# Hybrid attention and mixture-of-experts layer: the down weights' loads move to ScalarE's queue

## What is computed

```
gates  = softmax over the 4 largest router logits of each token, 0 elsewhere     (256 x 32)
for each expert e:                                    wgu 1024 x 2048, wd 1024 x 1024
    hgu  = xt @ wgu[e] + bgu[e]
    gate = min(hgu[:, :1024], 7);  up = clip(hgu[:, 1024:], -7, 7)
    y    = ((up + 1) * gate * sigmoid(1.702 * gate)) @ wd[e] + bd[e]
    acc += gates[:, e] * y
out = rmsnorm(h + acc)
```

## Time and profile before

| | |
|---|---|
| median of 3 runs | 1243.33 us (1241.56 to 1244.72) |
| the profiled execution | 1241.16 us, span 1239.3 us |
| TensorE matmuls busy | 1121.8 us (91% of the span) |
| VectorE, ScalarE, GpSimd busy | 205.8, 167.0, 18.6 us |
| bytes moved by DMA | 437.11 MB, mean 353 GB/s over the span |
| SyncE's queue | 434.19 MB; ScalarE's queue 1.57 MB |
| mean granted TensorE clock | 0.987 |

### The profile page before, as it was taken

How to read it: one execution, slowest core, us unless ns; L and a number is a source line. 1 busy time by engine, 2 the same in 40 slices (tenths; PEclk the granted TensorE clock), 3 DMA queues, 4 the chain that set the end, 5 groups by cost and what they waited for, 6 DMA issues and landing times.

```text
span 1239.3 us, 15513 instructions
## 1 busy us (share of the span) xinstructions
PE 1121.8 (91%) x6044; PEld 444.4 (36%) x6044; DVE 205.8 (17%) x420; ACT 167.0 (13%) x326; POOL 18.6 (1%) x68
## 2 busy tenths in 40 slices
PE   7999999958999999999999999999999998898885
PEld 6676444433333332323333233333333332322321
DVE  1301222141112111111111111111111111111111
ACT  2274222140000000000000000000000000000002
POOL 1010000000000000000000000000000000000000
PEclk9999999978999999999999999999999999999998
DMA  9922123338999999999999999999999999999994
GB/s 334 386 75 109 51 111 140 135 136 333 407 417 418 418 417 418 418 417 418 418 419 418 417 418 418 418 417 418 417 418 417 417 417 417 417 418 418 417 418 194
DMA packets 86628, 437.11 MB, mean 353 GB/s; under 512 B 7704, under 2 KB 7760, under 8 KB 53744
## 3 DMA queue, kind: packets, MB, share of 16 engines
q1 hardware_dynamic: 84880, 434.19, 86.3%
q10 hardware_dynamic: 1424, 1.57, 0.5%
q0 software_dynamic: 304, 1.06, 0.2%
HBM read 435.74 MB, written 1.06 MB: 352 GB/s over the span
## 4 chain that ended last, share of the span: by engine, by line
SPq 47%; PE 37%; DMA 9%; issue 4%; DVE 2%; ACT 1%; DVEq 0%
SPq L315 26%; SPq L310 20%; PE bank L1019 10%; DMA ring<-in_w_gate_up_dram 7%; PE bank L862 7%; PE bank L859 5%; PE bank L1049 3%; PE bank L945 2%; PE bank L956 2%; DMA ring<-in_w_down_dram 2%; PE bank L1002 2%; PE bank L993 1%; PE bank L917 1%; PE bank L839 1%; PE bank L1038 0%
## 5 line engine op out<-in xcount | busy, mean ns | idle before, releaser
L1019 PE MATMUL bank<-ring,gates 128*64 128x512 f32 x2048 | 476.9, 604 | 18.2 <-DMA ring<-in_w_gate_up_dram 15.3
L1049 PE MATMUL bank<-ring,gates 128*64 128x512 f32 x1024 | 244.2, 603 | 60.0 <-DMA ring<-in_w_down_dram 59.9
L1019 PEld LDWEIGHTS bank<-ring,gates 128*64 128x64 f32 x2048 | 135.1, 137 | 276.9 <-issue 191.3
L771 DVE TENSOR_SCALAR gates<-bank 128x512 f32<-128x512 f32 x32 | 22.1, 691 | 790.2 <-PE bank L1019 790.2
L1049 PEld LDWEIGHTS bank<-ring,gates 128*64 128x64 f32 x1024 | 64.0, 136 | 238.8 <-DMA ring<-in_w_down_dram 152.8
L862 PE MATMUL bank<-ring,colsT 128*128 128x512 f32 x192 | 85.0, 597 | 0.0
L1002 PE MATMUL bank<-gates,scatter_w 64*128 64x512 f32 x256 | 63.6, 615 | 0.8 <-ACT gates L570 0.7
L566 ACT ACTIVATE gates<-gates 128x512 f32<-128x512 f32 x32 | 20.2, 630 | 296.6 <-DVE gates L771 296.6
L859 PE MATMUL bank<-colsT,ring 128*128 128x256 f32 x256 | 58.8, 388 | 0.0
L993 PEld LDWEIGHTS bank<-onehot,qkT 128*128 128x128 bf16 x1536 | 47.7, 99 | 27.9 <-issue 25.2
L570 ACT ACTIVATE gates<-bank 128x512 f32<-128x512 f32 x32 | 19.1, 597 | 260.9 <-PE bank L1049 260.9
(11 more groups left out here) (167 smaller groups left out, 500.3 us busy)
## 6 DMA issues: line engine op xcount, KB each, us to landing
ring<-in_w_gate_up_dram SPq DMA_DIRECT2D x256, 1024.0 KB, 20.6
ring<-in_w_down_dram SPq DMA_DIRECT2D x128, 1024.0 KB, 24.6
ring<-in_w_in_dram SPq DMA_DIRECT2D x10, 2048.0 KB, 18.7
ring<-in_w_out_dram SPq DMA_DIRECT2D x1, 4096.0 KB, 14.1
ring<-in_w_proj_sb_dram SPq DMA_DIRECT2D x1, 2048.0 KB, 7.6
ring<-in_w_proj_moba_dram SPq DMA_DIRECT2D x1, 2048.0 KB, 13.4
resid<-in_x_dram SPq DMA_DIRECT2D x2, 512.0 KB, 3.7
bias<-u_scratch POOLq DMA_DIRECT2D x1, 1024.0 KB, 12.4
```

Source lines behind the costliest of these rows:

```text
L771: V.tensor_scalar(gate_t, bank[4][:, :], SWIGLU_LIMIT, None, ALU.min).then_inc(gate_rd, 1)
L1019: ins = mm(bank[4 + i][SLOTS * c:SLOTS * (c + 1), :], xeT[:, k, :], ring[:, k, i * D + c * CH:i * D + (c + 1) * CH], start=False, stop=k = ...
L1049: ins = mm(bank[6][SLOTS * c:SLOTS * (c + 1), :], rows, ring[:, KD + s, j * D + c * CH:j * D + (c + 1) * CH], start=k == 0, stop=k == KD - 1)
```

## The change

Down loads of experts 1 to 31 are issued by ScalarE, in its loop, behind `expert_rows` of the expert before. Four are issued one after the other, behind the copy of y, which itself waits for all four down slots. SyncE keeps expert 0's twelve loads and all gate-up loads. In a further pass, which doesn't happen with these data, SyncE would load expert 0's down weights as before. Two helpers with the slot and the source rows are shared by both engines.

```diff
+        dn = w_down[0].rearrange("e (k c p) n -> e k p c n", p=P, c=2)
+
+        def down_slot(s):
+            return ring[:, s, :].rearrange("p (c n) -> p c n", c=2)
+
+        def down_rows(e, s):
+            return (dn[e, s - KD] if isinstance(e, int)
+                    else dn[bass.ds(e, 1), s - KD].rearrange("o p c n -> p (o c) n"))
...
             def load_slot(e, s):
...
-                    dst = ring[:, s, :].rearrange("p (c n) -> p c n", c=2)
-                    src = (dn[e, s - KD] if isinstance(e, int)
-                           else dn[bass.ds(e, 1), s - KD].rearrange("o p c n -> p (o c) n"))
-                    sp.dma_start(dst, src).then_inc(slot_in[s], 16)
+                    sp.dma_start(down_slot(s), down_rows(e, s)).then_inc(slot_in[s], 16)
...
                 load_gate_up(1, done)
                 with sp.Fori(1, E - 1) as e:
                     load_gate_up(e + 1, done)
-                    load_down(e, done)
-                load_down(E - 1, done)
...
                     gate_sigmoid(e + done)
                     expert_rows(e + (done - 1))
+                    for s in range(KD, RING):
+                        act.dma_start(down_slot(s), down_rows(e, s)).then_inc(slot_in[s], 16)
                 hidden_columns(done + (E - 1))
```

More of the change, by code:

```diff
@@ L303, in _ @@
             gu = w_gate_up[0].rearrange("e (k p) n -> e k p n", p=P)
-            dn = w_down[0].rearrange("e (k c p) n -> e k p c n", p=P, c=2)
             def load_slot(e, s):
```

## The result

The changed kernel takes 1305.7 us (median of 4 runs, 1303.54 to 1308.78) against 1243.82: a ratio of 1.0499 (95% interval 1.0479 to 1.0520), 62 us slower. The profiled execution has a span of 1301.8 us, 62.5 more than before. Most of the loss lies where the prediction saw none, inside the periods.

What follows compares the result with a forecast made beforehand. The prediction took the saturated DMA engines (418 GB/s, 30.1 us an expert) as the bound. Its terms, 13.7 us at the end (1.4 of the first expert included) and 1 for the clock, summed to +14.7: 1258 us, range 1247 to 1285.

Steps and rivals of the forecast that it cites:

- ScalarE's issues: In each expert, ScalarE's four issues, some 2 us, vanish in its idle 6.5 us after copying y: cost 0.
- rival C: ScalarE's issues held up like SyncE's, 4.02 us each, delaying token weights: +97 us, 1355 us; chance 0.03.
- Later issue, no gap: Between 400 and 1214 us, later down issues cost 0, as four or five gate-up loads are still to come.
- step 3: Inside the periods, down loads get half the bandwidth beside gate-up loads and land in time: cost 0.
- rival A: Inside the periods, down loads get a third; 1 to 2.5 us lost in each of 27: 1285 to 1325 us; chance 0.12.
- twelve small gaps: TensorE's waits per expert, said to become one of 3 to 4 us before the last gate-up slot, without moving the period.
- The rate: DMA rate of the mixed stream stays at 418 GB/s, no change, with 1% either way (8 us of 814).
- Rival B: In the saturated stream, the rate rises, up to 434 GB/s: 30 us back over 27 periods, 1228 us; chance 0.10.
- First expert: At the first moved down loads, near 330 us, the DMA engines stand idle for 1.4 us: +1.4 us.
- Last expert: At the end, expert 31's down loads are asked for late, last landing 1235.7 instead of 1222.0: +13.7 us, first expert's term included.
- The 1 us added for a halved clock: In the tail, a gap before the last gate-up slot may halve TensorE's clock: 0 to 3.5 us, 1 taken.
- Rival D: Throughout the experts, SyncE's issuing is the bound and half its work moves away: 113 us less, 1145 us; chance 0.02.

Runs made afterwards that it cites:

- e4: Kernel before the change, all loads on SyncE's queue, but each expert's down loads wait until all four down slots are used: 1251.4 us, ratio 1.0053.
- e3: Changed kernel, but expert 31's down loads are issued by SyncE, slot by slot: 1299.4 us, ratio 1.0434.
- e8: Kernel before the change, all loads on SyncE's queue, with down rows of 8 KB instead of 4 KB: 1235.8 us, ratio 0.9937.
- e7: Changed kernel with four extra matmuls of constants, results unused, before the waits for down slots 2 and 3 each: 1268.0 us, ratio 1.0200.
- e9: Changed kernel with eight extra matmuls of constants per expert, results unused, all before gathering the next tokens: 1271.4 us, ratio 1.0242.

## Why the prediction was wrong

It forecast the right sign and too little: 1258 us, with a range to 1285. By its steps:

1. *ScalarE's issues*: right. 0.38 us each, behind a pause of 6.5 us before, and no stall of SyncE's kind (rival C) was seen.
2. *Later issue, no gap*: right by itself (e4). Its premise, that four or five gate-up loads are always outstanding, fell with step 3.
3. *The share*: this step failed, and its "Cost of the share 0" with it. The measured share is a third, as rival A had it, and the last down load of a long expert lands at S + 33.4 (770.5 - 737.1; the rival's figure to the tenth), so TensorE waits twice, both queues run empty, and 31.9 us go for an expert instead of 30.1. "That is a good half" was a wrong reading of the earlier trace rows. It set 175 GB/s against the 308 of the slice from 15 to 20 us, but the three loads landed at 18.5 to 21.5 us, and until about 16.4 us none of their rows was moved. From 16.4 to 20.4 us the trace of before has, for ScalarE's queue (q10) and SyncE's (q1):

```profile
q10 hardware_dynamic: 123, 0.73, 73.6%
q1 hardware_dynamic: 124, 0.25, 25.6%
```

   0.73 of 0.98 MB are three quarters, with ScalarE's rows of 8 KB and SyncE's of 2 KB: linked as above, the packets show mostly one or two short rows between two long ones, where turns of equal bytes would need four. The row that was held against rival A was itself a case of row turns, and it was carried over to loads whose rows have the opposite ratio.
   The Trainium skill's packet rule (DMA: Bandwidth & Descriptors, Queues, rings and completion order), as I read it, gave turns of equal bytes and the half. The four spacings and the packet counts above differ from that: here a turn is mostly one row, of 2, 4 or 8 KB.

   A smaller slip stands in the same step: the "twelve small gaps" of an expert are 4.5 in the earlier trace rows (97 + 25 in 27 experts). Nothing in the sum hangs on it.
4. *The rate*: 418 where the stream ran; the mean fell to 396 by the holes. Rival B's idea was sound only in part: 422 GB/s came, but from 8 KB rows, on one queue as on two.
5. *First expert*: right. The flow dips once, where 418 GB/s ran before:

```profile
328.00:330.00 2.00, 2.00 (x14) 0.83 (x12) 0.00 (x0) 0.60 (x1) 0.00 (x0) 1.00 0.57 184
330.00:332.00 2.00, 2.00 (x12) 0.45 (x8) 0.00 (x0) 0.00 (x0) 0.00 (x0) 1.00 0.95 362
```

   That is 2 x (234 + 56) / 418 = 1.4 us, as forecast.
6. *Last expert*: right. 13.7 with step 5 is 12.3 without it, and 12.7 were measured. The mechanism held: 14.0 us from the first issue at 1270.55 to the last landing for 12.6. That 8 of these 12.7 us are TensorE's backlog, which stays when the slots are asked for one by one, was in the sum but not in its words, and misled me once more in e3. The 1 us added for a halved clock did not come: the granted clock was 1.00 from 1250 to 1272 us.

Rival A's price, 1285 to 1325, holds the result; 1 to 2.5 us a period were forecast and 31.9 - 30.1 = 1.8 lost. So the terms that made up the sum of 14.7 us held, and nearly all of the 47 us above them come from the one step that had been put at 0. What rival A's chance of 0.12 lacked was a closer look at the one row that it was weighed by. Rival D is refuted by its own sign: SyncE's queue went from 47% of the chain to 0 and the kernel got slower.

## What to carry to other kernels

Two DMA queues that feed one consumer don't share by bytes or by need: on this chip each engine took turns by row, so the stream with the shorter rows got the smaller part, and a load that is needed first may come last. Keep loads on one queue in the order of use when the DMA engines are saturated (e8, with 8 KB rows, is the fastest kernel here); if there must be two queues, give both rows of the same length, and long ones (1246 us with 8 KB, 1273 with 4 KB). A queue that looks busy for 4 us a load may only be full; test it with an issue of the same line into an empty queue.

## What was unexpected in the hardware

- Row turns hold for ratios of the rows from 2:1 to 1:4, to within 3% (3.8, 5.0, 7.4, 12.2 us a megabyte).
- The rate of a saturated stream went with the length of its rows: all 8 KB rows 422 GB/s, two thirds of the bytes in 8 KB and the rest in 4 KB 418, the other way round 413, all 4 KB 409.
- Useless work made the kernel faster by 34 to 38 us (e7, e9): with it the two-beat rhythm of 26 and 37 us evened out and the holes went. Whether the pace alone did it or the clock had a part stays open.
